# RWKV pass: four projection steps per scan chunk, one per half level, and an inverse on left columns

## What is computed

```python
def step(S, inp):
    r_t, w_t, k_t, v_t, a_t, b_t = inp
    sa = jnp.einsum('bhij,bhj->bhi', S, a_t)
    S = S * w_t[:, :, None, :] + sa[..., None] * b_t[:, :, None, :] + v_t[..., None] * k_t[:, :, None, :]
    return S, jnp.einsum('bhij,bhj->bhi', S, r_t)
...
h = jnp.concatenate([x, dx], axis=-1) @ w_comb
r, k, v, g, w_lo, a_lo = jnp.split(h, list(np.cumsum(widths)[:-1]), axis=-1)
w = -jax.nn.softplus(-(w0 + jnp.tanh(w_lo) @ w2)) - 0.5
a = jax.nn.sigmoid(a0 + a_lo @ a2)
```

## Time and profile before

| | us |
|---|---|
| median of 3 runs | 2376.39 |
| lowest, highest | 2374.34, 2379.22 |
| profiled execution | 2373.65 |
| its span | 2371.9 |
| TensorE busy in it | 2295.2 |
| mean granted clock (share) | 0.987 |

### The profile page before, as it was taken

How to read it: one execution, slowest core, us unless ns; L and a number is a source line. 1 busy time by engine, 2 the same in 40 slices (tenths; PEclk the granted TensorE clock), 3 DMA queues, 4 the chain that set the end, 5 groups by cost and what they waited for, 6 DMA issues and landing times.

```text
span 2371.9 us, 51852 instructions
## 1 busy us (share of the span) xinstructions
PE 2295.2 (97%) x22065; PEld 1789.5 (75%) x22065; DVE 1235.5 (52%) x2284; ACT 851.7 (36%) x1762; POOL 1142.6 (48%) x771
## 2 busy tenths in 40 slices
PE   8999999999999999999999999999899999999898
PEld 7788787788887677777777777777688887777776
DVE  4353278577804555555555555555421566556511
ACT  4122112233302445555555555555221343343300
POOL 4555566866763434443444333344356344344245
PEclk9999999999999999999999999999799999999899
DMA  3333233233322312222222222221523322121212
GB/s 111 89 80 78 83 90 88 80 98 98 108 98 64 92 57 72 69 66 66 66 66 70 72 66 66 66 66 56 183 68 114 105 70 61 41 61 52 83 58 93
DMA packets 263757, 188.07 MB, mean 79 GB/s; under 512 B 18267, under 2 KB 242393, under 8 KB 263145
## 3 DMA queue, kind: packets, MB, share of 16 engines
q1 hardware_dynamic: 263529, 184.76, 26.0%
HBM read 162.69 MB, written 22.04 MB: 78 GB/s over the span
## 4 chain that ended last, share of the span: by engine, by line
PE 61%; DVE 2%; POOL 1%; DMA 1%; issue 1%; ACT 0%; SPq 0%; POOLq 0%; DVEq 0%
PE ps L1348 18%; PE ps L159 7%; PE ps L160 6%; PE ps L161 6%; PE ps L1510 3%; PE ps L1526 3%; PE ps L1552 2%; PE ps L2388 2%; PE ps L1466 1%; PE ps L1499 1%; PE ps L1438 1%; PE ps L1361 1%; PE ps L221 1%; DMA z_lo<-z_kept 1%; PE ps L2374 1%; PE ps L1483 1%
## 5 line engine op out<-in xcount | busy, mean ns | idle before, releaser
L150 POOL TENSOR_TENSOR w_lo<-raw,w_hi 128x1024 fp32r<-128x1024 f32 (+1 forms) x196 | 494.8, 2524 | 16.4
L147 POOL TENSOR_SCALAR w_hi<-raw 128x1024 fp32r<-128x1024 f32 (+1 forms) x196 | 217.1, 1108 | 559.1 <-PE ps L161 542.1
L159 PE MATMUL ps<-h_hi,w_hi 128*128 128x512 f32 x616 | 244.2, 396 | 5.7 <-POOL w_lo L150 4.6
L161 PE MATMUL ps<-h_hi,w_lo 128*128 128x512 f32 x616 | 240.9, 391 | 0.0
L160 PE MATMUL ps<-h_lo,w_hi 128*128 128x512 f32 x616 | 240.4, 390 | 0.0
L1885 POOL TENSOR_TENSOR kp<-k_b,kp 128x528 f32<-128x528 f32 x16 | 29.6, 1847 | 362.0 <-ACT kp L1647 362.0
L1348 PE MATMUL ps<-mixed_r,raw 128*64 128x264 f32 x1024 | 154.4, 391 | 2.3 <-ACT g_b L1589 2.3
L159 PEld LDWEIGHTS ps<-h_hi,w_hi 128*128 128x128 f32 x616 | 116.3, 189 | 31.9 <-POOL w_lo L150 7.2
L1348 PE MATMUL ps<-mixed_k,raw 128*64 128x264 f32 x1024 | 138.3, 389 | 0.0
L161 PEld LDWEIGHTS ps<-h_hi,w_lo 128*128 128x128 f32 x616 | 115.9, 188 | 24.8
L160 PEld LDWEIGHTS ps<-h_lo,w_hi 128*128 128x128 f32 x616 | 116.2, 189 | 23.2
(11 more groups left out here) (447 smaller groups left out, 5862.1 us busy)
## 6 DMA issues: line engine op xcount, KB each, us to landing
raw<-in_rwkv_w_in_dram SPq DMA_DIRECT2D x64, 512.0 KB, 4.0
raw<-in_w_up_dram SPq DMA_DIRECT2D x44, 512.0 KB, 3.9
raw<-in_w_in_dram SPq DMA_DIRECT2D x41, 512.0 KB, 3.8
raw<-in_w_down_dram SPq DMA_DIRECT2D x22, 512.0 KB, 3.5
raw<-in_mla_w_in_dram SPq DMA_DIRECT2D x22, 512.0 KB, 4.0
sb_kept<-xT SPq DMA_DIRECT2D x16, 528.0 KB, 3.0
xT<-sb_kept SPq DMA_DIRECT2D x16, 528.0 KB, 4.2
raw<-in_rwkv_w_out_dram SPq DMA_DIRECT2D x16, 512.0 KB, 4.5
```

The costliest lines, as they stand in the source:

```text
L147: nc.gpsimd.tensor_scalar(w_hi[s][:, 0:width], raw[s][:, 0:width], 1.0, 0.0, ALU.mult, ALU.add).then_inc(split_hi, 1)
L150: nc.gpsimd.tensor_tensor(w_lo[s][:, 0:width], raw[s][:, 0:width], w_hi[s][:, 0:width].bitcast(F32), ALU.subtract).then_inc(split_ready, 1)
L159: nc.tensor.matmul(dst, w[0], x[0], start=start, stop=False)
L161: return nc.tensor.matmul(dst, w[1], x[0], start=False, stop=stop)
```

## The change

- `FILL_S` becomes (1, 2, 1): 36 steps stand in the scan. `FILL_X` and `FILL_T` become 1 each, `FILL_END` 5. The total stays 68.
- ScalarE copies items 3 to 6 in chunks 5 to 8, and item 7 before gn_square.
- A level changes the left columns of each pair of blocks only (block size 2^lv). The X and T matmuls have 32 moving columns (H) for 64, with `left` picking and `packed` placing them; `x_m` and `lv_pad` have half the width, `x_m` also a third slot of zeros. VectorE adds into the left columns of `t_m`; the transposes stay whole.
- In level 5 VectorE copies all of `t_t` into `tb` (two instructions) between the two products and the T results, and then copies the new quarter blocks into place (four) where it added before (four). `tl_ev` counts 6 a pass.
- In pass 0 ten small copies and a memset prepare `lv_pad` and `x_m`, for two copies before.

```diff
-        FILL_S = (1, 1, 1)
-        FILL_TURN, FILL_GRAM, FILL_FIRST, FILL_END = 4, 8, 5, 4
-        FILL_X, FILL_T = (2, 2, 2, 2, 2), (2, 2, 2, 2, 2)
+        FILL_S = (1, 2, 1)
+        FILL_TURN, FILL_GRAM, FILL_FIRST, FILL_END = 4, 8, 5, 5
+        FILL_X, FILL_T = (1, 1, 1, 1, 1), (1, 1, 1, 1, 1)
...
+        def left(ap, lv):
+            s = 1 << lv
+            if len(ap.shape) == 2:
+                return ap.rearrange("p (a t s) -> p a t s", t=2, s=s)[:, :, 0, :]
+            return ap.rearrange("p m (a t s) -> p m a t s", t=2, s=s)[:, :, :, 0, :]
...
-        SCAN_ITEMS = {2: (0,), 3: (1,), 4: (2,), 6: (3,), 7: (4,), 8: (5,)}
+        SCAN_ITEMS = {2: (0,), 3: (1,), 4: (2,), 5: (3,), 6: (4,), 7: (5,), 8: (6,)}
...
-                                mm = nc.tensor.matmul(ps[own[h], 2 + p, x * C:x * C + C], mb[:, c0 + x, own[h]], t_m[:, c0 + x, :],
-                                                      start=True, stop=True)
+                                mm = nc.tensor.matmul(packed(ps[own[h], 2 + p, x * H:x * H + H], lv), mb[:, c0 + x, own[h]],
+                                                      left(t_m[:, c0 + x, :], lv), start=True, stop=True)
...
-                                dst = ps[own[h], 4 + p, x * C:x * C + C]
+                                dst = ps[own[h], 4 + p, x * H:x * H + H]
...
-                                    mm = nc.tensor.matmul(dst, x_m[:, c0 + x, h, :], t_t[:, c0 + x, :], start=True, stop=True)
+                                    both = x_m[:, c0 + x, h:h + 2, :].rearrange("p a b -> p (a b)")
+                                    mm = nc.tensor.matmul(dst, both, t_t[:, c0 + x, H:C], start=True, stop=True)
...
             if B:
                 turned()
-            if A:
-                item(6)
             if B:
                 scan_weights()
+            if A:
+                item(7)
             if Cs:
                 gn_square()
             if B:
                 inverse_blocks(0)
             if A:
-                item(7)
                 factors_a()
...
+                if lv == 5:
+                    dve.wait_ge(tb_ev, 8 * b + 8)
+                    for h in range(2):
+                        nc.vector.tensor_copy(tb[own[h], :, own[h]], t_t[own[h], :, :]).then_inc(tl_ev, 1)
+                    dve.wait_ge(tl_ev, 6 * b + 2)
...
-                        nc.vector.tensor_tensor(t_m[:, c0:c0 + m, :], part_of(4 + p, m), t_m[:, c0:c0 + m, :],
-                                                ALU.add).then_inc(tadd_ev, 1)
+                        grown = left(t_m[:, c0:c0 + m, :], lv)
+                        nc.vector.tensor_tensor(grown, packed(part_of(4 + p, m), lv), grown, ALU.add).then_inc(tadd_ev, 1)
...
-                            nc.vector.tensor_tensor(tb[own[h], c0:c0 + m, own[h]], part_of(4 + p, m)[own[h], :, :],
-                                                    t_t[own[h], c0:c0 + m, :], ALU.add).then_inc(tl_ev, 1)
+                            nc.vector.tensor_copy(tb[C * h:C * h + H, c0:c0 + m, C * h + H:C * h + C],
+                                                  part_of(4 + p, m)[C * h:C * h + H, :, :]).then_inc(tl_ev, 1)
```

More of the change, by code:

```diff
@@ L1247, in program @@
         t_m = put("t_m", [P, NC_, C])
-        x_m = put("x_m", [P, NC_, 2, C])
+        H = C // 2
+        x_m = put("x_m", [P, NC_, 3, H])
         t_t = put("t_t", [P, NC_, C])
@@ L1259, in program @@
         assert put.end <= LV_PAD, put.end
-        lv_pad = region(LV_PAD)("lv_pad", [P, 5, 2, C])
+        lv_pad = region(LV_PAD)("lv_pad", [P, 5, 2, H])
         assert LV_PAD + 2.5 <= 147.75
@@ L1309, in chunks, with packed @@
             return buf[:].rearrange("p (a b) -> p a b", b=C)
+        def left(ap, lv):
[3 more added lines that the diff above has]
+            return ap.rearrange("p m (a t s) -> p m a t s", t=2, s=s)[:, :, :, 0, :]
+        def packed(ap, lv):
+            s = 1 << lv
+            if len(ap.shape) == 2:
+                return ap.rearrange("p (a s) -> p a s", s=s)
+            return ap.rearrange("p m (a s) -> p m a s", s=s)
         def halves_of(buf, at=PAD):
@@ L1390, in wo_unit @@
                     elif m == 2:
-                        pe.wait_ge(tl_ev, 4 * PAIRS)
+                        pe.wait_ge(tl_ev, 6 * PAIRS)
                         pe.wait_ge(gn_ln, PAIRS - 1)
@@ L1446, in pass_pe @@
                     if n == 0:
-                        pe.wait_ge(tl_ev, 4 * c + 4)
+                        pe.wait_ge(tl_ev, 6 * c + 6)
                     for h in range(2):
@@ L1755, in decay_scan @@
             nc.vector.tensor_tensor_scan(lsum[:], restart[:], ws_b[:], 0.0, ALU.mult, ALU.add).then_inc(scanned, 1)
-        EARLY_PADS, MIDDLE_PADS, PADS = 6, 14, 20
+        EARLY_PADS, MIDDLE_PADS, PADS = 6, 14, 29
         def early_pads(dve):
@@ L1780, in late_pads @@
             nc.vector.memset(lv_pad[:], 0.0).then_inc(pads, 1)
-            dve.wait_ge(pads, PADS - 2)
-            for h in range(2):
-                nc.vector.tensor_copy(lv_pad[own[h], :, h, :], lv_mask[own[h], 1:6, :]).then_inc(pads, 1)
+            nc.vector.memset(x_m[:, :, 2, :], 0.0).then_inc(pads, 1)
+            dve.wait_ge(pads, PADS - 10)
+            for lv in range(1, 6):
+                for h in range(2):
+                    nc.vector.tensor_copy(packed(lv_pad[own[h], lv - 1, h, :], lv), left(lv_mask[own[h], lv, :], lv)).then_inc(pads, 1)
         def pass_dve(dve, i, A, B, Cs):
@@ L1829, in part_of @@
             def part_of(bank, m):
-                return ps[:, bank, 0:m * C].rearrange("p (a b) -> p a b", b=C)
+                return ps[:, bank, 0:m * H].rearrange("p (a b) -> p a b", b=H)
             def level(lv):
@@ L1834, in level @@
                     dve.wait_ge(x_mm, 10 * b + (2 * (lv - 1) + p + 1))
-                    nc.vector.tensor_tensor(x_m[:, c0:c0 + m, :, :], part_of(2 + p, m).unsqueeze(2).to_broadcast([P, m, 2, C]),
-                                            lv_pad[:, lv - 1, :, :].unsqueeze(1).to_broadcast([P, m, 2, C]),
+                    nc.vector.tensor_tensor(x_m[:, c0:c0 + m, 0:2, :], part_of(2 + p, m).unsqueeze(2).to_broadcast([P, m, 2, H]),
+                                            lv_pad[:, lv - 1, :, :].unsqueeze(1).to_broadcast([P, m, 2, H]),
                                             ALU.mult).then_inc(x_ev, 1)
+                if lv == 5:
+                    dve.wait_ge(tb_ev, 8 * b + 8)
+                    for h in range(2):
+                        nc.vector.tensor_copy(tb[own[h], :, own[h]], t_t[own[h], :, :]).then_inc(tl_ev, 1)
+                    dve.wait_ge(tl_ev, 6 * b + 2)
                 for p, (c0, m) in enumerate(PARTS):
@@ L1893, in pass_pool @@
                 if Cs:
-                    pool.wait_ge(tl_ev, 4 * c + 4)
+                    pool.wait_ge(tl_ev, 6 * c + 6)
                 held(pool)
```

## The result

| us | before | after |
|---|---|---|
| median (4 runs each) | 2375.36 | 2420.81 |
| lowest, highest | 2373.66, 2379.22 | 2419.9, 2424.41 |
| profiled execution | 2373.65 | 2424.41 |
| its span | 2371.9 | 2422.7 |

A forecast was written before the change was run, and what follows sets the result against it. TensorE, busy for 97% of the span, was taken to bound the kernel. The terms -23.7 + 0 + 0 + 32.4 + 11.8 + 0 + 5 = +25.5 us on 2376.4 gave 2402 us, range 2363 to 2412.

The forecast's parts named there:

- The signs that the prediction named: Timeline marks: level matmuls 29 ns, idle about 2.2 us, P 1.67 us after S, cycle 2.64, half levels 1.50, pass 58.8.
- Part 1: Scan chunks: a second step fills TensorE's wait for the copy of U; 1.7 us gained a pass, -23.7 us.
- Part 2: Level matmuls with half the moving columns: still 29.1 ns each, bound by the weight load; 0 us.
- The rival of faster matmuls: Levels: weight loads hide, a pair takes 34 ns and VectorE bounds a level; 2366 us, 12 in 100.
- Part 3: Levels: one step per half level instead of two gives 1.50 us, VectorE's halved products keep up; 0 us.
- Part 4: FIRST: the first step of g waits 2.16 us for ScalarE's copy of v, in passes 1 to 15; +32.4 us.
- Part 5: Scan chunk 4: the step for the second half of a waits for ScalarE's copy; +0.84 a pass, +11.8 us.
- Part 6: End of a pass: VectorE's new copies, 0 taken from 0 to +0.7 us; pad copies in pass 0 at most +1.
- Part 7: TensorE's clock falling to half after the new 2.16 us idle: 3 falls taken, +5 us, bounds 0 and 25.
- The rival of a late clock: VectorE's end-of-pass copies held up behind GpSimd, or clock loss at its upper end; 2412 to 2430, 15 in 100.

## Why the prediction was wrong

The signs that the prediction named came out, or nearly, in a pass at full clock (28.3 ns, a wait of 2.04 us, P 1.72 us after S, a cycle of 2.63, half levels of 1.50, a pass of 58.86). None of them looked at the clock, and there it failed.

- **Part 1** held: -1.7 us a pass forecast, 55.73 - 57.47 = -1.74 measured once the waits were gone (this holds parts 2 and 3 too). (14 x 1.7 is 23.8, not 23.7; nothing hangs on it.)
- **Part 2** held: 29.1 ns for a narrow level matmul was taken, 28.3 measured, and a pass of 57.47 us with narrow columns alone. The rival of faster matmuls is out (its 34 ns for a pair was worked out from no row; 2 x 13.5 is 27). That the weight load bounds them fits: a pair takes 56.6 ns, and 56 was worked out from the earlier trace rows for its load. The Trainium skill, "TensorE: Matmul & The Clock Gate", LDWEIGHTS (loading the stationary operand), says that the load goes by the columns of the weights; the 53 ns that the prediction estimated from it for 64 columns lie just below the pair.
- **Part 3** held: half levels of 1.50 us, and the experiment with full columns shows the cover that it spoke of: without the shorter products, a level takes 3.24 us.
- **Part 4** was sized at 2.16 us a pass and is 2.26 by the pass's length. The step from a queue order and one chain of ScalarE to a wait was right to 0.1 us.
- **Part 5**: 0.84 forecast, 0.87 measured.
- **Part 6** failed in a small thing: "the ten small pad copies in pass 0 replace two: at most +1 us once". They take 5.30 us for 0.99, and TensorE's sums wait behind them: +4.2 us. Three of the ten were held for 1.26 us beside GpSimd; the prediction had this mechanism in a rival, for the 64 x 576 copies, and not here. The two 64 x 576 copies at the pass's end cost nothing, as taken. (Its sum for the moment at which the scan's first copy is wanted gives X + 6.46, not 6.4.)
- **Part 7** is the step that made the prediction wrong: "I take 3 falls: +5 us", for 25.5 us measured. The value lies at the end of its bounds, 0 to 25. The choice inside them rested on one idle of 2.76 us without a fall, and the range went only 10 us above the forecast, so it gave the upper bound almost no weight. No row about a single idle could have decided it: the same 2.04 us gave 0, 5, 9 or 13 falls in 14 passes, and that very idle of 2.76 us was followed by a stretch at half clock in five of twelve profiles. The price of one fall was too low as well: 1.7 us was taken, and six of nine cost 1.6, one 3.2 and two 6.4, in the mean 2.8. The rival of a late clock, 2412 to 2430, was the one that came true, for its second reason and not for the late VectorE; it had 15 in 100.

With 4.2 for the pads and 25.5 for the clock in the places of 0 and 5 the forecast's sum gives +50 for the profiled execution's 50.8. That the other executions are 4 us faster (2419.9 to 2420.8) I can't split: their clock means are 0.976 to 0.977 for 0.975.

## What to carry to other kernels

When steps are moved along a queue, follow each one to the wait that comes with it: both new waits came from the copies of other steps that had not moved along, and both went by moving one copy each into idle time that ScalarE had. A wait of some 2 us that comes in every pass must be priced with the falls of the clock behind it, and the range must hold everything from no fall to a fall in every pass: here they added 25 us to the 46 that both waits cost, and an edit elsewhere in the pass turned them on or off. Where new VectorE instructions are put in, look at what GpSimd does at that moment: beside it three copies of 0.18 us became 1.26 us each.

## What the runs showed of the hardware

- An idle of 2.04 us on TensorE was followed by a stretch at 1.2 GHz in 0, 5 or 9 of 14 passes, with passes of 58.0, 58.74 and 58.86 us, and in 13 of 14 with passes of 60.26 us. An idle of 2.76 us in unchanged code was followed by one in 5 of 12 profiles. Idles of 0.6 and 0.8 us were followed by none in 14, and so was the 2.04 us wait when 1.79 us of it were filled with unused matmuls.
- Being busy doesn't bring the clock back at once: in two passes TensorE stayed at 1.2 GHz for 13.6 us while it was busy for all of them, with the levels' narrow matmuls and one step after each group.
- Moving one copy of 0.47 us (that of a0) by a chunk changed the time by 33 us, of which 12 were waited for.
- A VectorE copy of 64 x 32 elements took 0.18 us, and 1.26 us in three of ten cases, each of which ended 0.03 or 0.04 us after the GpSimd instruction beside it. Two copies of 64 x 320 took 0.48 us each beside a GpSimd instruction and were not held.
- A level matmul with 32 moving columns takes 28.3 ns. The Trainium skill, "TensorE: Matmul & The Clock Gate", Back-to-back issue gap, gives about 25 for the closest two small matmuls can start; here the weights change with each, and the trace stays above it.
